# Where the first experts' weights are put, and in which order the first gathers and the first expert unit run

## The reference

```python
def layer_norm(x, w, b):
    xf = x.astype(jnp.float32)
    xc = xf - jnp.mean(xf, axis=-1, keepdims=True)
    var = jnp.mean(xc * xc, axis=-1, keepdims=True)
    return (xc * lax.rsqrt(var + LN_EPS) * w + b).astype(x.dtype)

def clamped_swiglu(h):
    glu, lin = jnp.split(h, 2, axis=-1)
    glu = jnp.minimum(glu, 7.0)
    lin = jnp.clip(lin, -7.0, 7.0)
    return glu * jax.nn.sigmoid(1.702 * glu) * (lin + 1.0)

def hybrid_layer(x, ...):                 # x: 256 tokens x 1024
    y_a, y_b, y_c, y_d = ...              # four mixers on slices of x @ w_in
    mix = jnp.sum(gates * branch_out, axis=2) @ w_out
    h = layer_norm(DEEPNORM_ALPHA * x + mix, ln1_w, ln1_b)
    top_val, top_idx = lax.top_k(h @ router_w + router_b, 4)      # 32 experts
    top_w = jax.nn.softmax(top_val, axis=-1)
    # for every token, over its 4 experts e:
    #   ffn += top_w[e] * (clamped_swiglu(h @ w1[e] + b1[e]) @ w2[e] + b2[e])
    return layer_norm(DEEPNORM_ALPHA * h + ffn, ln2_w, ln2_b)
```

## Time and profile before

| | us |
|---|---|
| median of 3 runs | 1284.54 (1284.0 to 1285.64) |
| span of the profiled execution | 1282.2 |
| TensorE busy in the span | 1242.3 (97%) |
| VectorE, ScalarE busy | 452.2 (35%), 219.6 (17%) |
| bytes moved by DMA | 458.70 MB, mean 358 GB/s |
| granted TensorE clock, mean | 0.998 |

### The profile page before, as it was taken

The page is one execution under the profiler, slowest core; times in us unless marked ns, Lnnn a source line. Parts: engine busy times, 40 slices in busy tenths (PEclk is TensorE's granted clock), DMA queues, the critical chain, the costliest instruction groups (busy, mean ns, idle before and its releaser), DMA issues.

```text
span 1282.2 us, 14909 instructions
## 1 busy us (share of the span) xinstructions
PE 1242.3 (97%) x6126; PEld 643.6 (50%) x6126; DVE 452.2 (35%) x914; ACT 219.6 (17%) x430; POOL 3.5 (0%) x17
## 2 busy tenths in 40 slices
PE   9999999999999999999999999999998999899996
PEld 8888888998873343333333333333323333333332
DVE  5999924556342512121321213212121312122123
ACT  1722124231040110101111010110101010110102
POOL 0000000000000000000000000000000000000000
PEclk9999999999999999999999999999999999999999
DMA  9534344336979999999999999999999999999996
GB/s 380 204 134 152 109 154 160 114 110 223 424 280 408 429 432 426 435 431 429 433 429 434 432 429 433 429 434 432 429 433 429 434 430 430 433 428 428 428 424 260
DMA packets 31486, 458.70 MB, mean 358 GB/s; under 512 B 4785, under 2 KB 5169, under 8 KB 9426
## 3 DMA queue, kind: packets, MB, share of 16 engines
q1 hardware_dynamic: 27728, 453.00, 84.2%
q10 hardware_dynamic: 3714, 5.07, 1.2%
HBM read 457.01 MB, written 1.05 MB: 357 GB/s over the span
## 4 chain that ended last, share of the span: by engine, by line
PE 74%; DMA 16%; DVE 7%; ACT 1%; issue 1%; DVEq 0%; SPq 0%; POOL 0%; POOLq 0%
PE banks L1333 20%; PE banks L910 15%; PE banks L1369 14%; DMA store<-in_moe_w 13%; PE banks L1341 4%; PE banks L924 4%; DMA store<-in_w_last 3%; PE banks L1160 2%; PE banks L1185 2%; DVE store L2057 2%; PE banks L1440 2%; PE banks L1249 2%; PE banks L1351 1%; DVE store L2054 1%; DVE store L2051 1%; DVE store L2056 1%
## 5 line engine op out<-in xcount | busy, mean ns | idle before, releaser
L1333 PE MATMUL banks<-store 128*64 128x512 f32 x1536 | 342.6, 595 | 16.7 <-DMA store<-in_moe_w 16.6
L1333 PEld LDWEIGHTS banks<-store 128*64 128x64 f32 x1536 | 109.4, 137 | 231.9 <-issue 205.7
L1369 PE MATMUL banks<-store 128*64 128x512 f32 x952 | 210.9, 595 | 0.0
L910 PE MATMUL banks<-store 128*128 128x256 f32 x896 | 196.8, 380 | 0.0
L910 PEld LDWEIGHTS banks<-store 128*128 128x128 f32 x896 | 169.3, 190 | 26.4 <-issue 3.9
L2051 DVE TENSOR_SCALAR store<-banks 128x512 f32<-128x512 f32 x32 | 22.1, 692 | 428.8 <-PE banks L1341 428.8
L1369 PEld LDWEIGHTS banks<-store 128*64 128x64 f32 x952 | 65.9, 137 | 142.8 <-issue 120.1
L1341 PE MATMUL banks<-store 128*64 128x512 f32 x512 | 116.8, 598 | 0.4 <-DMA store<-in_moe_w 0.4
L2065 DVE COPY store<-banks 64x512 f32<-64x512 f32 x30 | 20.8, 694 | 203.3 <-PE banks L1369 203.3
L789 ACT ACTIVATE store<-store 128x512 f32<-128x512 f32 x28 | 17.6, 630 | 431.0 <-DVE store L2051 431.0
L1341 PEld LDWEIGHTS banks<-store 128*64 128x64 f32 x512 | 34.3, 136 | 70.1 <-issue 67.7
(11 more groups left out here) (380 smaller groups left out, 842.3 us busy)
## 6 DMA issues: line engine op xcount, KB each, us to landing
store<-in_moe_w SPq DMA_DIRECT2D x72, 4096.0 KB, 30.3
store<-in_moe_w SPq DMA_DIRECT2D x36, 2048.0 KB, 14.7
store<-in_w_in SPq DMA_DIRECT2D x30, 1024.0 KB, 4.8
store<-in_moe_w SPq DMA_DIRECT2D x18, 1024.0 KB, 9.3
store<-in_w_branch SPq DMA_DIRECT2D x8, 1024.0 KB, 4.8
store<-in_w_out SPq DMA_DIRECT2D x4, 1024.0 KB, 6.0
store<-in_w_last SPq DMA_DIRECT2D x4, 1024.0 KB, 34.8
store<-in_w_first SPq DMA_DIRECT2D x4, 256.0 KB, 4.3
```

The costliest lines, as they stand in the source:

```text
L910: last = mm(b[:, j * SEQ:(j + 1) * SEQ], w[:, k, j * P:j * P + P], xT[:, k, :], start=k == 0, stop=k == KD - 1)
L1333: last = mm(bank[into[i]][64 * ct:64 * ct + 64, :], xg[:, 2 * c + kk, col:col + CAP], w[:, kk, i * FF + ct * 512:i * FF + ct * 512 + 512], ...
L1369: last = mm(bank[4][64 * dh:64 * dh + 64, :], actT[:, j, 64 * fh:64 * fh + 64], w[j][:, 512 * dh:512 * dh + 512], start=(fh, j) == (0, 0), ...
```

## The change

`ln_w`, the copy of ln1_w for all 128 partitions in `spare`, is dropped, and both halves of `spare` are loaded in one 1 MB transfer behind unit 6. Unit 10 is the *guest* (`GUEST`): its first 1 MB goes to `x_res`, whose contents are not needed between x_hat and the experts' sums, one half after each half of x_hat; its second 1 MB goes to the first half of unit 0's place. `second_layer` reads it from both. The second half of unit 0's place stays empty until unit 20.

`normed` moves to after expert 1, since `x_res` holds weights until then. ln1_w now comes as one row beside `b2_all`; TensorE copies it to all partitions by two one-row matmuls into PSUM (`weight_row`), and VectorE multiplies from there, in four products of 512 columns.

TensorE's order is new around the first unit: the gathers of blocks 0 to 5 come first, unit 0 starts its sums itself, and the bias and the gathers of blocks 6 and 7 follow unit 0. ScalarE takes blocks 0 to 3 in pairs (`xg_early`); the blocks' places in PSUM change for that. The waits for the router's small tensors are merged into one.

```diff
@@ -64,6 +64,7 @@
 HOME = 3
 BIAS_PAIR = 11
 APART = 3 * NU - 1
+GUEST = 2 * NDBL
...
@@ -99,6 +100,8 @@
 COMB_BANK = (6, 7, 2, 3)
 LOGIT_BANK = (4, 4)
 RANK_BANK = (3, 5)
+NORM_BANK = (6, 5)
+ROW = 64
...
         vec = spare[:, D + 4 * P:D + 4 * P + NVEC + S5T]
-        ln_w = spare[:, 0:D]
...
             if k in (1, 2):
                 return bank[5 + k][:, 0:P]
-            if k == 5:
-                return bank[4][:, 0:P]
-            return bank[2 + k // 4][:, (k % 4) * P:(k % 4 + 1) * P]
+            if k in (3, 5):
+                return bank[(5, 4)[k // 5]][:, 0:P]
+            return bank[3 if k == 4 else 2][:, (k % 4) * P:(k % 4 + 1) * P]
...
@@ -434,6 +436,7 @@
             sp.wait_ge(S["acc_ready"], 4)
             load(4)
             load(6)
+            sp.dma_start(spare[:, 0:2 * D], unit_source(2, NU - 1)[:, SLOT:UNIT]).then_inc(S["apart_landed"], 16)
             sp.wait_ge(S["chunk_used"], used_up("wo", 1))
...
             sp.wait_ge(S["chunk_used"], used_up("wo", 3))
             load_part(8, 1).then_inc(unit_landed[4], 16)
             load_part(9, 0).then_inc(unit_landed[5], 16)
-            sp.dma_start(spare[:, D:2 * D], unit_source(2, NU - 1)[:, SLOT + D:UNIT]).then_inc(S["apart_landed"], 16)
-            for i in range(2):
-                for part in (slice(0, FF), slice(FF, 2 * FF)) if i == 0 else (slice(0, 2 * FF),):
-                    sp.wait_ge(S["half_used"], part.stop // FF + i)
-                    e, c = HEAD[2 * NDBL + i]
-                    sp.dma_start(unit_at(2 * NDBL + i)[:, part], unit_source(e, c)[:, part]).then_inc(S["half_landed"], 16)
-                sp.wait_ge(S["expert_chunk_used"], i + 1)
-                load_part(2 * NDBL + i, 1).then_inc(double_landed[NU // 2 - 1], 16)
-            sp.wait_ge(S["ln_used"], 2)
-            sp.dma_start(spare[:, 0:D], unit_source(2, NU - 1)[:, SLOT:SLOT + D]).then_inc(S["apart_landed"], 16)
+            for half in range(2):
+                sp.wait_ge(S["x_hat_ready"], 4 * half + 4)
+                sp.dma_start(x_res[:, half, :], unit_source(*HEAD[GUEST])[:, D * half:D * half + D]).then_inc(S["half_landed"], 16)
+            for j in range(2):
+                sp.wait_ge(S["half_used"], j + 1)
+                sp.dma_start(unit_at(GUEST)[:, D * j:D * j + D], unit_source(*HEAD[GUEST])[:, SLOT + D * j:SLOT + D * j + D])\
+                    .then_inc(double_landed[NU // 2 - 1] if j else S["half_landed"], 16)
+            sp.wait_ge(S["half_used"], 3)
+            load_part(GUEST + 1, 0).then_inc(S["half_landed"], 16)
+            sp.wait_ge(S["expert_chunk_used"], 2)
+            load_part(GUEST + 1, 1).then_inc(double_landed[NU // 2 - 1], 16)
...
+            act.dma_start(rb, A["router_b"].to_broadcast([P, NE])).then_inc(S["rw_in"], 16)
             act.dma_start(x_res, A["x"][0].rearrange("(h p) n -> p h n", p=P)).then_inc(S["xres_in"], 16)
-            act.dma_start(ln_w, A["ln1_w"].to_broadcast([P, D])).then_inc(S["ln_in"], 16)
...
             def gathered(g, first=False):
 
-                act.wait_ge(S["xg_first"], g + 1)
                 for k in range(KD):
-                    if k == 4:
+                    if first and k in (0, 2):
+                        act.wait_ge(S["xg_early"], k // 2 + 1)
+                    elif k == (4 if first else 0):
+                        act.wait_ge(S["xg_first"], g + 1)
+                    elif k == (6 if first else 4):
                         act.wait_ge(S["xg_psum"], g + 1)
...
             act.dma_start(b2_all[0:NE, :], A["moe_b2"]).then_inc(S["b_in"], 16)
             act.dma_start(b2_all[NE:NE + 1, :], A["ln1_b"]).then_inc(S["b_in"], 16)
+            act.dma_start(b2_all[ROW:ROW + 1, :], A["ln1_w"]).then_inc(S["b_in"], 16)
...
             mm(bank[RANK_BANK[1]][:, 0:NE], earlier[:, :], member[:, 1, :], start=False, stop=True).then_inc(S["rank_psum"], 1)
-            pe.wait_ge(S["b_in"], 16 * 4)
-            bias(0)
             pe.wait_ge(S["sel_ready"], 1)
             for k in range(3):
                 pe.wait_ge(S["x_hat_ready"], 5 + k)
-                first_gather(1, (k,))
+                last = first_gather(1, (k,))
+                if k == 1:
+                    last.then_inc(S["xg_early"], 1)
             first_gather(0, (3,))
             pe.wait_ge(S["x_hat_ready"], 8)
-            first_gather(1, (3,)).then_inc(S["xg_first"], 1)
-            first_gather(1, (4, 5))
-            for k in (6, 7):
-                first_gather(0, (k,))
-                last = first_gather(1, (k,))
-            last.then_inc(S["xg_psum"], 1)
+            first_gather(1, (3,)).then_inc(S["xg_early"], 1)
+            first_gather(1, (4, 5)).then_inc(S["xg_first"], 1)
...
                 if c == NW1:
-                    pe.wait_ge(S["half_landed"], 48)
+                    pe.wait_ge(S["half_landed"], 64)
...
@@ -1363,6 +1366,8 @@
                     w = [whole[:, D * j:D * j + D] for j in range(4)]
                     if last_apart and c == NU - 1:
                         w[2:] = [spare[:, D * j:D * j + D] for j in range(2)]
+                    if guest and c == NW1:
+                        w = [x_res[:, j, :] for j in range(2)] + w[0:2]
...
+            def weight_row():
+
+                pe.wait_ge(S["b_in"], 16 * 7)
+                for dh in range(2):
+                    mm(bank[NORM_BANK[dh]][:, :], ones[ROW:ROW + 1, :], b2_all[ROW:ROW + 1, 512 * dh:512 * dh + 512],
+                       start=True, stop=True, tile_position=(ROW, 0)).then_inc(S["weight_row"], 1)
+
...
-            first_layer(first_unit, 0, 0, returned=((0, 0), (0, 1), (1, 1)))
+            first_layer(first_unit, 0, 0, cs=(0,), returned=((0, 0), (0, 1)), fresh=True)
+            pe.wait_ge(S["b_in"], 16 * 4)
+            bias(0, fresh=False)
+            for k in (6, 7):
+                first_gather(0, (k,))
+                last = first_gather(1, (k,))
+            last.then_inc(S["xg_psum"], 1)
+            first_layer(first_unit, 0, 0, cs=(1, 2, 3), returned=((1, 1),))
             bias(1, (2, 3))
             first_layer(second_unit, 1, 0, into=(2, 3), cs=(0, 1), returned=((0, 1), (1, 1)))
...
-            second_layer(second_unit, 1, turn=False)
+            second_layer(second_unit, 1, turn=False, guest=True)
+            weight_row()
             gather(1, range(4))
...
             def third_unit(c):
 
+                if c == 1:
+                    pe.wait_ge(S["normed_used"], 2)
                 if c == 2:
-                    pe.wait_ge(S["apart_landed"], 16 * 5)
+                    pe.wait_ge(S["apart_landed"], 16 * 4)
...
-            def normed(half):
-
-                dve.wait_ge(S["x_hat_ready"], 4 * half + 4)
-                x_hat_columns = h_tok[:, half, :].rearrange("p (c k q) -> p c q k", k=4, q=P)
-                V.tensor_tensor(every_column(x_res[:, half, :]), x_hat_columns, every_column(ln_w), ALU.mult).then_inc(S["ln_used"], 1)
-                dve.wait_ge(S["ln_used"], half + 1)
+            def normed(dh):
+
+                dve.wait_ge(S["weight_row"], dh + 1)
+                for half in range(2):
+                    ins = V.tensor_tensor(y_acc[:, half, 512 * dh:512 * dh + 512].rearrange("p (q k) -> p q k", k=4),
+                                          h_tok[:, half, 512 * dh:512 * dh + 512].rearrange("p (k q) -> p q k", k=4),
+                                          bank[NORM_BANK[dh]][:, :].rearrange("p (q k) -> p q k", k=4), ALU.mult)
+                ins.then_inc(S["normed_used"], 1)
 
             V.tensor_scalar(small[:, 232:234].unsqueeze(2), top[:, :, 0:1], -1.0, None, ALU.mult).then_inc(S["topexp_req"], 1)
-            dve.wait_ge(S["ln_in"], 16)
-            normed(0)
-            normed(1)
...
-            V.memset(wTd[NE:NE + 1, :, :], ALPHA).then_inc(S["ln_used"], 1)
+            V.memset(wTd[NE:NE + 1, :, :], ALPHA)
             dve.wait_ge(S["at_psum"], 2)
             list_items(item_ef, True)
             second_out(1, 1)
+            normed(0)
+            normed(1)
             list_items(item_off, False)
```

More of the change, by code:

```diff
@@ L270, in encoder_layer @@
         stream_total = [16 * sum(1 for i in range(1, len(STREAM)) if i % R1 == c) for c in range(R1)]
-        names = """apart_landed half_used half_landed logit_read ln_used chunk_used const_ready iota_made vec_in s5_in lru_in pos_in ones_ready s5_small s5_mag s5_theta s5_trig0 c_in cT_ready f_ready trig_ready bu_psum bu_free x_ready x_used
+        names = """apart_landed half_used half_landed logit_read chunk_used weight_row normed_used const_ready iota_made vec_in s5_in lru_in pos_in ones_ready s5_small s5_mag s5_theta s5_trig0 c_in cT_ready f_ready trig_ready bu_psum bu_free x_ready x_used
             y_evac gelu_ready glu_psum glu_gate gate_sum yC_ready proj_evac xc_ready gate_psum gate_act soft_in soft_out sp_ready
@@ L739, in _ @@
             act.wait_ge(S["yA_ready"], 2)
[L740 removed]
+            act.dma_start(ln1_cols[:, :], A["ln1_cols"]).then_inc(S["rw_in"], 16)
```

(21 more changed lines are left out.)

6 lines of the change are left out of this document (2 added, 4 removed).

## The result

The changed kernel takes 1288.01 us (median of 12 runs, 1286.8 to 1289.42), the kernel before in the same call 1284.63 (12 runs, 1283.86 to 1285.99). The ratio is 1.0024 [1.0016 to 1.0032]: 3.4 us slower, with 2.1 to 4.1 us for the interval. That is above the predicted range. The profiled execution took 1288.39 us, its span 1286.4, against 1282.2 before. It ran 0.39 us late already at the router's load (issued at 366.05 after, 365.66 in the earlier trace rows).

The account below looks back on a forecast made before the run. Transfers were taken to bound the kernel, through loads waiting for places TensorE gives back. The early-load saving was spent in waiting: span 1282.2 + 0.25 = 1282.45, plus 2.3 to the median, 1284.8 us, range 1282.4 to 1286.6.

Parts of the forecast that it names:

- The gap: Transfers near 384 to 387 us: an old gap closes and a new one of about 4.1 us opens.
- TensorE's order: Around the first unit: 0.75 us idle for the selection, first unit 1.1 us earlier, everything from unit 1 on 0.75 us later.
- The fixed cost of a load: A load that meets idle engines takes 2.3 us besides its bytes at 432 GB/s; 4 MB needs 12.0 us.
- the credit of 3.64 us: 1.5 MiB loaded early around the router, at 432 GB/s; the saving would be spent in waiting for places.
- The weight row: Two one-row matmuls after expert 1, 4 instructions, taken as 1.8 us of TensorE.
- TensorE's lateness: From the third expert on, TensorE 2.55 us late: 0.75 from the order plus 1.8 from the weight row.
- Unit 12: 2 MB load issued at 389.49 before, landing at 401.3; forecast at 397.5, the stream at most 3.8 us ahead.
- against 12.0 for idle engines it had 2.3 us of other transfers ahead of it: The 4 MB load issued at 483.40, landing 14.3 us later, was read as having 2.3 us of backlog.
- the stream is there +0.25 us: At the 4 MB load of 483.40: issued at 485.95, landing no sooner than 497.95, so 0.25 us later to the end.
- B: Rival, 22 in 100: weight row priced like the packed bias, TensorE 1.3 us late, part of the gap stays closed; 1283.2 us.
- C: Rival, 12 in 100: the whole credit of 3.64 us is kept, the backlog near 483 us being misread; 1280.9 us.
- D: Rival, 7 in 100: VectorE's four products take 2.8 us each, TensorE waits 3.0 us in the third expert; 1287.7 us.

Follow-up runs that it names:

- both runs with less work: Biases of experts 1 and 2 left out of the computation, once with the early loads (-1.36 us), once in the kernel before (-0.48 us).
- The 4 MB load that was held back: The kernel before with one 2 MB and one 4 MB load held back until the engines are empty; single run, 1300.22 us.
- both back: The changed kernel with expert 0's bias back in the wait, without the weight row and the products with ln1_w; +0.18 us, 1.0003 against the kernel before.
- less work, early loads: The changed kernel, expert 0's bias back in the wait, weight row at pair 11, biases of experts 1 and 2 left out; 0.9988 of the kernel before.

## Why the prediction was wrong

**Right.** What bounds the kernel: transfers, and in these kernels only what is lost before about 510 us moves the end; in ten of the eleven kernels of the table the rest of the span is 774.7 to 775.8 us. The gap: almost nothing moved from 384 to 386 us, and the next load, issued at 385.88 (forecast 385.1), met idle engines and took 4.7 us. TensorE's order: 0.73 us of idle time for 0.75, the first unit 1.1 us earlier net of the offset. The fixed cost of a load. VectorE's products: 3.90 us for 4, hidden. That the credit of 3.64 us would be spent in waiting for places.

**Mis-sized.** The weight row took 1.98 us, not 1.8. Unit 1 came 1.07 us later, not 0.75: the gathers in two pieces take 1.83 + 1.16 = 2.99 us where one run of 22 took 2.72. TensorE's lateness was 3.05 us and not 2.55. The second 0.5 MB was issued at 380.19 and landed at 385.1, not at 379.8 and 383.3. Unit 12 landed net 1.4 us earlier, not 3.8: the step left out the 1 MB load of 387.60 that stands ahead of it.

**The step that failed** is "against 12.0 for idle engines it had 2.3 us of other transfers ahead of it", and with it "the stream is there +0.25 us". The reading of 14.3 - 12.0 is a time by which one load alone may slip; the step took it as a time by which the stream may slip at no cost. The table shows what happens in place of it. Where the lead of this load was 4.6 us or more (before, and both runs with less work), it and its successor came 19.4 us after the predecessor, which is the full rate (8.39 MB in 19.4 us, 432 GB/s). Where it was 2.6 to 3.7 us, above the 2.3 that should do, seven of eight kernels took 20.2 to 21.4 us: 0.8 to 2.0 us were lost, though the load came before the engines were empty by that arithmetic. The kernel after shows such losses at four more places from 391 to 476 us, unit 12 among them, each 1.1 to 1.5 us at a lead of 2.8 to 3.7; two others of that kind lost nothing. So the kernel before stood on the edge, and 1.98 us more of TensorE cost 1.86.

The DMA packets in the traces show part of how. A load ends on each of the 16 engines with a packet of 4 bytes, and it has landed when the last of them is through. In the kernel before, the first engine was through with the predecessor 1.34 us after the load of the earlier trace rows was issued, the last 4.17 us after. In the kernel after it was 0.61 and 3.02 us, and 11 of the 16 were through within 1.0 us. The 4 MB load that was held back put its first packet on idle engines 0.96 us after its issue (501.02), and 15 of its first 16 packets of 32 KB took 1.56 to 2.07 us, where a packet in the full stream takes 1.22. In the first 4.5 us behind the issue of the load of the earlier trace rows 3 packets took over 1.5 us in the kernel before, 13 in the kernel after, and 10 to 15 in the eight kernels of the shorter leads. So what the kernel before had in hand is, by an estimate from these numbers, 1.34 - 0.96 = 0.4 us and not 2.3: beyond it one engine after another meets the new load idle. The 8 us behind the issue, before and after, in the columns of the earlier trace rows:

```profile
484.00:492.00 8.00, 8.00 (x36) 2.51 (x34) 0.10 (x1) 0.00 (x0) 0.00 (x0) 1.00 1.01 426
487.00:495.00 8.00, 8.00 (x36) 2.51 (x34) 0.54 (x1) 0.44 (x1) 0.00 (x0) 1.00 0.97 385
```

The same reading tells where the credit of the early bytes went. A stream that is ahead of TensorE has a shorter lead, as its loads still wait for the same places. In "both back" the predecessor landed 0.8 us earlier (487.15 - 365.61 against 488.02 - 365.66), the lead fell from 4.64 to 3.44, and the two next loads took 2.0 us more.

With the lateness put down in full, the sum would have been 1284.5 + 3.05 = 1287.6 us, 0.4 under the measured median. The rivals fared no better. B's row price was wrong, C's reading of the backlog was wrong in the other direction, and D came nearest in time, 1287.7, by luck, as its mechanism isn't there: TensorE does not wait for VectorE in the third expert.

**Open.** The packets explain the size of a loss only in part: one kernel lost nothing at a lead of 3.53, though 11 of its packets were slow (and "less work, early loads" nothing at 4.74 with 8), others 1.4 at 3.34 and 3.64. Why a first packet is slow, and why the engines end a load up to 3 us apart, isn't shown. Losses at a long lead occur too (1.0 us at 440.28 in the kernel before, lead 7.66). The order alone costs 0.65 us in the kernel before, and putting the bias back brings 1.85 in the changed one; the intervals overlap.

## What to carry over

Where transfers bound a kernel and wait for places that another engine gives back, a new instruction on that engine ahead of them was paid nearly in full here (1.86 for 1.98 us), though some microseconds of queue seemed to hide it; the same instructions near 1012 us cost nothing that could be told. Read how long before its predecessor's landing each load is issued, and when the first of the 16 engines is through with that predecessor: the time in hand goes by the first engine, not by the landing. Bytes loaded earlier gained nothing by themselves while the places came free no earlier (+0.18 us).

## What the runs showed that was not expected

- A matmul of one row by 512 columns in f32 costs about what one of 33 rows does: 1.98 us for 4 instructions, 0.50 each, beside 0.46 with 33 rows (3.70 for 8).
- In seven of eight kernels two 4 MB loads lost 0.8 to 2.0 us at a lead of 2.6 to 3.7 us, while a load alone lands 7.2 and 12.2 us after its issue, with only 2.3 to 2.5 us beyond its bytes at 432 GB/s.
- After one wait of 3.13 us TensorE's granted clock was about 0.5 (from 1020 to 1030 us), and 8 matmuls took 7.19 us in place of 3.7.
